# Value products ahead of the probability transposes in the attention loop of a two-layer diffusion step

## The reference

```
h = LN(x) * (1 + scale1) + shift1
u = h @ W_in                       -> neighbourhood attention (4 heads x 64), short convolution,
                                      differential attention (4 heads, two 64-wide maps, 128-wide values)
x = LN_affine(alpha * x + gate1 * (concat(A, B, C) @ W_out))
x = LN_affine(alpha * x + gate2 * MoE(LN(x) * (1 + scale2) + shift2))

differential head:   p = softmax(q k / 8) for two maps;  a = p0 - lambda * p1;  o = a @ v
neighbourhood head:  p = softmax(q k / 8 + bias over a window, context keys);   o = p @ v
```

## Time and profile before

| | us |
|---|---|
| median of 3 runs | 1045.84 (1038.78 to 1047.57) |
| the profiled execution | 1043.02 |
| its span, first to last instruction | 1041.1 |
| TensorE busy in the span | 793.1 (76%) |
| VectorE, ScalarE busy | 351.3 (34%), 213.5 (21%) |
| attention stage, layer 0 | 174.6 to 253.9 |
| attention stage, layer 1 | 683.6 to 762.8 |

### The profile page before, as it was taken

The page is one execution under the profiler, slowest core; times in us unless marked ns, Lnnn a source line. Parts: engine busy times, 40 slices in busy tenths (PEclk is TensorE's granted clock), DMA queues, the critical chain, the costliest instruction groups (busy, mean ns, idle before and its releaser), DMA issues.

```text
span 1041.1 us, 14052 instructions
## 1 busy us (share of the span) xinstructions
PE 793.1 (76%) x4044; PEld 507.6 (49%) x4045; DVE 351.3 (34%) x796; ACT 213.5 (21%) x513; POOL 109.2 (10%) x161
## 2 busy tenths in 40 slices
PE   3899998878992597878519999977899526799820
PEld 2675554545872343534218655544478514345400
DVE  1101102754576221212083010056527661122127
ACT  0320002444000022212123100044510102122210
POOL 0310100000010110102143000000000111000020
PEclk9899999999995699999759999989999558999965
DMA  9962395486063899798283422328420369954241
GB/s 378 369 241 82 120 399 218 189 344 235 5 224 148 339 424 360 255 404 274 63 343 144 162 81 84 119 71 331 197 81 1 141 238 422 424 222 149 80 135 68
DMA packets 39798, 222.94 MB, mean 214 GB/s; under 512 B 5008, under 2 KB 5840, under 8 KB 22832
## 3 DMA queue, kind: packets, MB, share of 16 engines
q1 hardware_dynamic: 19008, 155.50, 38.2%
q0 software_dynamic: 12240, 50.22, 13.5%
q10 hardware_dynamic: 8480, 16.33, 4.4%
HBM read 194.70 MB, written 27.33 MB: 213 GB/s over the span
## 4 chain that ended last, share of the span: by engine, by line
PE 58%; DVE 13%; issue 10%; DMA 6%; PEld 5%; ACT 3%; PEldq 2%; ACTq 1%; POOL 1%; POOLq 0%; DVEq 0%; SPq 0%
PE psum L508 18%; PE psum L638 7%; PE psum L505 7%; PE psum L647 6%; PE psum L593 4%; PE psum L668 3%; PEld psum L593 3%; PE psum L679 3%; DMA big<-in_weights 3%; PE psum L625 2%; PE psum L457 2%; DMA shared<-h_rows,gcol 2%; PE psum L613 2%; DVE mxs L1235 1%; PE psum L520 1%
## 5 line engine op out<-in xcount | busy, mean ns | idle before, releaser
L508 PE MATMUL psum<-big 128*128 128x384 f32 x576 | 190.9, 488 | 2.7 <-issue 2.7
L508 PEld LDWEIGHTS psum<-big 128*128 128x128 f32 x576 | 108.6, 190 | 78.6 <-issue 8.3
L647 PE MATMUL psum<-big,shared 128*64 128x256 f32 x576 | 75.1, 419 | 20.1 <-issue 17.4
L1547 DVE TENSOR_SCALAR shared<-shared 128x128 f32<-128x128 f32 (+1 forms) x28 | 7.0, 251 | 235.5 <-ACT shared L1033 235.5
L593 PE MATMUL psum<-big 128*128 128x256 f32 x384 | 83.9, 380 | 2.0 <-ACT big L969 1.8
L593 PEld LDWEIGHTS psum<-big 128*128 128x128 f32 x384 | 72.6, 190 | 12.9 <-issue 3.2
L638 PE MATMUL psum<-big,shared 128*128 128x512 f32 x160 | 71.0, 597 | 7.9 <-issue 7.9
L505 PE MATMUL psum<-big 128*128 128x256 f32 x288 | 69.5, 402 | 7.6 <-DMA big<-in_weights 3.9
L457 PE MATMUL psum<-const,big 128*128 128x128 f32 x160 | 31.4, 309 | 51.9 <-ACT big L859 28.4
L647 PEld LDWEIGHTS psum<-big,shared 128*64 128x64 f32 x576 | 48.8, 151 | 43.6 <-issue 27.1
L505 PEld LDWEIGHTS psum<-big 128*128 128x128 f32 x288 | 57.6, 203 | 18.2 <-ACT big L866 7.5
(11 more groups left out here) (229 smaller groups left out, 898.0 us busy)
## 6 DMA issues: line engine op xcount, KB each, us to landing
big<-in_weights SPq DMA_DIRECT2D x80, 1024.0 KB, 7.5
big<-in_experts SPq DMA_DIRECT2D x22, 2048.0 KB, 14.1
big<-in_experts SPq DMA_DIRECT2D x22, 1024.0 KB, 10.9
moe_rows<-ln_b POOLq DMA_DIRECT2D x3, 3584.0 KB, 25.5
moe_rows<-shared ACTq DMA_DIRECT2D x20, 256.0 KB, 5.6
moe_rows<-shared ACTq DMA_DIRECT2D x36, 128.0 KB, 7.5
ln_b<-in_ln POOLq DMA_DIRECT2D x4, 1024.0 KB, 6.4
gate_b<-mod_rows POOLq DMA_DIRECT2D x4, 1024.0 KB, 7.4
```

The costliest lines, as they stand in the source:

```text
L508: ins = pe.matmul(bank(name)[:, 0:T], w[piece][:, k, part * P:(part + 1) * P], hT[:, k, :], start=(k == 0), stop=(k == KC - 1))
L647: ins = pe.matmul(psD[HALF * j:HALF * j + HALF, 0:DE], xT[:, k * P:k * P + HALF], w[:, 2 * DE * k + DE * j:2 * DE * k + DE * j + DE], star ...
```

## The change

In the loop over the steps the call of `attend` for the step behind moves from after `prob_transposes` to before it. TensorE's list in step i becomes S(i+2), A(i-1), T(i). The modulation vector, the head transposes and every other engine's list stay where they are, and so do the buffers and the number of instructions.

```diff
                 for i, (kind, h, t) in enumerate(STEPS):
                     if i + 2 < N_STEPS:
                         score(L, i + 2)
+                    if i > 0:
+                        attend(L, i - 1)
                     prob_transposes(L, i)
                     if i > 0:
-                        attend(L, i - 1)
                         if STEPS[i - 1][0] == "da" and STEPS[i - 1][2] == 2:
                             mod_vector(L, 2 + STEPS[i - 1][1])
```

## The result

The changed kernel takes 1049.46 us (median of 9 runs, 1046.62 to 1054.79) beside 1042.29 for the kernel before on the same chip (9 runs, 1036.72 to 1047.57): ratio 1.0070, 95% interval 1.0045 to 1.0095. It is 7.2 us slower where 1.4 us faster was forecast. That 1049.46 still lies inside the range of 1038 to 1050 is luck: the range was set for a kernel before of 1045.84, whose median over more runs came out 3.6 us lower, and the sum's own worst end was 2.7 us slower. The profiled execution took 1048.27 us with a span of 1046.3. Medians and ranges here are of all runs, while a ratio leaves out runs over 1.5% above the fastest of their kernel, so the two can differ.

A forecast was written before the change was run, and what follows sets the result against it. No engine is full, so waits set the attention stage; six terms sum to 0.7 us gained per layer, 1.4 in both, off the median 1045.84: forecast 1044.4 us, range 1038 to 1050.

The forecast's parts named there:

- term 6: Stage's end: T(23) waits behind A(22), T(21) slips behind A(20); loss of 0.64 to 1.44 us a layer, 0.9 taken.
- term 1: Stage's start: A(0) fills T(1)'s wait, so S(4) and S(5) come earlier; gain 0.17 to 0.57 us a layer, 0.35 taken.
- another low-clock stretch: Sign of being wrong: the low-clock stretch at the stage's start gets longer or another appears; no size given.
- 2 vector of step 9: Modulation vector of step 9 stands behind T(9) alone and starts earlier; gain 0.44 to 0.70 us a layer, 0.55 taken.
- 3 vector of step 12: Modulation vector of step 12 likewise starts earlier, after copy(12); gain 0.53 to 0.79 us a layer, 0.6 taken.
- 4 head transposes: Head transposes of step 15 start earlier, though A(14) pushes T(15) by 0.24; gain 0.46 to 0.70 us, 0.5 taken.
- Term 5: Neighbourhood steps 14 to 22: changed costs between operation shapes; -0.7 to +1.5 us a layer over nine, loss of 0.4 taken.
- The rival of the open copy: Neighbourhood steps: exponentials delay the copy, A(i) waits 0.57 us a step, 13.7 us over both layers, 1059.5 us; chance 7%.
- shrank to 12.6 us and not to 8: Sign: TensorE's waits for probabilities before the transposes, over both layers, should shrink from 20.8 us to about 8.

The follow-up runs named there:

- second of the kernels with fillers in part 4: Changed kernel with old order in steps 16, 19 and 22, plus 22 identity transposes before T(0) and 12 before the first head transposes: 1045.59 us, ratio 1.0003.
- Both kernels with fillers in part 4: 22 and 12 idle-time identity transposes added to new order in steps 1 to 15 only (1034.31 us), or everywhere except steps 16, 19, 22 (1045.59 us).
- first-part kernel: Changed kernel with the new order in steps 1 to 15 only, old order from step 16: 1038.73 us, ratio 0.9971 to the kernel before.

## Why the prediction was wrong

**The step that failed** is the sentence that "the moved product never waits where the transposes would not have", since both need only the copy that frees slot D. The first product of a neighbourhood head also claims slot E, which head_out of the head behind must free. What was on record had both: the old order at step 22 lists `free_E` at A(21) (the list of the new order starts at A(21) and shows only `free_D` on it, but the trace has the wait), and term 6 says that head_out stands behind copy(21) on ScalarE. In the old order T(22) stood between and hid it. Opened, it costs 0.54 and 0.81 us a layer, 1.06 at the end of the stage.

**The sum had no term for the clock.** With the slot waits, TensorE does 11.38 us of work in 14 where it did 12.55, and the clock falls for 10 us: 1.36 us in the stage (19.85 - 18.49) and 2.72 in the out projection, which the prediction never priced since it is not touched. Both layers: 8.2 us, the measured loss and more; filling the waits with work that nobody needs gave 7 us back. The short low stretch takes another 0.74 us a layer (term 1 below), which the gain of 1.74 has already paid. The prediction named another low-clock stretch as what would make it wrong, and put no chance on it, although already showed one behind a wait. The Trainium skill, "TensorE: Matmul & The Clock Gate", section "A second HAM failure mode: psum-queue depth-cycling", tells of a kernel whose short idle times between groups of matmuls made the clock go to and fro; the trace agrees in part, with one fall behind waits of 0.81 us and less in either layer.

Term by term, layer 0, times from S(0):

| term | predicted | measured | from |
|---|---|---|---|
| 1 start | +0.35 | +0.67 at the first head transposes | 31.07, 30.40 |
| clock, short stretch | none | -0.61 by T(9) | 6.77, 7.38 |
| 2 vector of step 9 | +0.55 | +0.78 | T(9) to L471: 1.45, 0.67 |
| 3 vector of step 12 | +0.60 | +0.46 | gain 0.84 to 1.30 |
| 4 head transposes | +0.50 | +0.44 | gain 1.30 to 1.74 |
| 5 and 6, without the slot | -1.30 | -0.99 | 17.43 - 16.44 |
| slot E | none | -1.06 | 18.49 - 17.43 |
| clock, stage | none | -1.36 | 19.85 - 18.49 |
| clock, out projection | none | -2.72 | 44.77 - 42.05 |

The rows of terms 1 to 4: row maximum after S(5), first head transposes, T(9), the vectors of steps 9 and 12, the last head transposes.

```profile
186.41 0.96 DVE L1236 TENSOR_REDUCE mxs<-psum 128x2 f32<-128x768 f32 x1 [0.86 <-PE psum L534]
...
204.15 0.55 PE L457 MATMUL psum<-const,head 128*128 128x128 f32 x3 [1.61 <-DVEq L1153]
...
211.53 0.30 PE L457 MATMUL psum<-const,big 128*128 128x128 f32 x1 [0.35 <-issue]
...
212.20 3.66 PE L471 MATMUL psum<-big,condT 128*32 128x256 f32 x64 [0.37 <-ACT big L950]
...
223.90 3.66 PE L471 MATMUL psum<-big,condT 128*32 128x256 f32 x64 [0.66 <-ACT big L950]
...
234.83 0.55 PE L457 MATMUL psum<-const,head 128*128 128x128 f32 x3 [0.37 <-ACT big L950]
```

From the first head transposes to T(9), layer 0: the changed kernel, then the second of the kernels with fillers in part 4, in the columns of the earlier trace rows.

```profile
204.15:211.53 7.38, 7.04 (x35) 4.48 (x36) 5.14 (x14) 4.42 (x15) 0.00 (x0) 0.77 0.95 395
```

```profile
203.78:210.42 6.64, 5.70 (x38) 3.54 (x36) 4.46 (x14) 4.42 (x15) 0.00 (x0) 1.00 0.97 405
```

- Term 1: the row maximum comes 13.32 - 12.66 = 0.66 us earlier after S(0) (the earlier trace rows for before), a little over the range, and at the first head transposes all of it is still there: 0.67 (0.40 in layer 1). It is lost behind them. From there to T(9) it takes 7.38 us for 6.77 (7.39 for 6.77 in layer 1), and the short low-clock stretch lies in between. Both kernels with fillers in part 4 have TensorE busy ahead of these transposes, keep the clock up and take 6.64 us for the same way, in both layers. So the short stretch costs 7.38 - 6.64 = 0.74 us a layer.
- Why that stretch appears: the vector of step 6, for which the prediction took nothing, starts 25.13 us after S(0) for 26.35. The head transposes behind it wait for VectorE's list, which has gained only half of that, so TensorE waits 1.61 us for 1.06. In all twelve layers traced with the new order there and no filler the wait is 1.52 to 1.63 us and the clock falls behind it; in all ten with the old order it is 1.05 or 1.06 and the clock stays up.
- Terms 2 to 4 hold in their mechanism: the vectors start when their copies are out, 0.05 and 0.34 us after the copies' ends (212.15 and 223.56; 0.1 to 0.4 was forecast). Each size falls just outside of its own range, one above and two below, and their sum, 1.68, is the forecast's 1.65 with some luck. All four terms and the short stretch give 1.74 for 2.0, and over both layers the first-part kernel got 3 us of that in its time.
- Term 5: a full neighbourhood step takes 2.11 us from transposes to transposes (236.09 to 238.20), and from T(20) in the earlier trace rows to T(21) it was 2.11 as well (245.90 to 248.01), so a full step loses nothing, where the prediction took a loss of 0.4 over nine steps. The Trainium skill, "TensorEngine Tiling (Array Packing)", section Tiling Modes, says that a change of tiling mode drains TensorE. Both orders change mode equally often, so by that rule the term is nothing, and the trace agrees with 2.11 us in either order.
- Term 6: with the slot out of the way the end loses 0.99, and the prediction's 0.9 stands.
- The rival of the open copy was wrong in its place: in the middle steps no value product waits for its copy. It is open at A(22) and A(23) alone, as term 6 said, and at 0.37 for A(21) once the slot is free.
- The waits before the transposes shrank to 12.6 us and not to 8, and that says little of the time: what counts is what the wait turns into.

Without the slot's wait and the fall at the end the terms leave 1.74 - 0.99 = 0.75 us a layer. That it is the forecast's 0.7 is luck, since it holds the short stretch, without which it would be 1.49. The sign was lost with one claim on one slot, and the size with the clock behind it.

## What to carry to other kernels

When a consumer moves ahead of a producer on an in-order engine, list everything that the moved work claims, the slot it writes as well as the operand it reads, and for each claim who frees it and behind what that stands in its own engine's list. A string of waits under a microsecond, shortly before a long run of matmuls, is to be priced by what the clock would cost in that run, not by its own length; one cure here was on another engine's list (ScalarE reads the head out first, 8 to 10 us), the other leaves the old order at the three steps in question (11 to 12 us).

## What was not expected of the hardware

- The clock went from the upper to the lower level for 10 us after waits of 0.54, 0.81 and 0.58 us with work between them, in both layers; the same waits left it up in one layer of one execution, so a kernel's own waits don't settle it alone.
- It fell for about 3 us behind a wait of 1.52 to 1.63 us in twelve layers of twelve, and behind one of 1.05 or 1.06 at the same place in none of ten. Work that starts earlier on TensorE can make the wait behind it longer (1.61 us for 1.06), and so the clock lower.
- It also stood at 0.51 for 21 us with TensorE busy for 19.93 of them, with waits of 0.37 us and less in the 5 us ahead, which left it up in another kernel.
- 14 transposes a layer that nobody reads, 2.0 us of work (0.84 + 0.60 + 0.60) in time that was idle, kept it up and were worth 7 us.
